# Group norms applied as they finish, and seven weight units inside a differential attention

## The reference, cut to what matters

```python
out_a = fox(...)   # causal softmax attention with forget gates, 4 heads of 64
out_b = mla(...)   # multi-head latent attention
out_c = stick(...) # stick-breaking attention
out_d = swa(...)   # sliding window, ALiBi, sinks
mix = concat([out_a, out_b, out_c, out_d])           # 4 groups of 256
y = group_rmsnorm(mix, mix_g) @ w_o                  # each group by its own rms
x = layernorm(ALPHA * x + y); x = layernorm(ALPHA * x + ffn(x))
```

```python
h = x + 0.5 * swiglu(rms_norm(x))
q, k, v, sc_b, sc_c, sc_x, lru_x, lru_g = split(rms_norm(h) @ w_in)
attn = softmax(q1 k1 + bias) - lam * softmax(q2 k2 + bias)   # 4 heads, 2 maps each
y_da = rms_norm(attn @ v, subln_g) * (1 - lam_init)          # each head by its own rms
y_sc = sc_b * causal_conv(sc_c * sc_x)
y_lru = gelu(lru_g) * rg_lru(conv(lru_x))                    # sigmoid gates, a scan over tokens
h = h + concat([y_da, y_sc, y_lru]) @ w_out
x = h + 0.5 * swiglu(rms_norm(h))
```

## Time and profile before

| | |
|---|---|
| median of 3 runs | 3333.64 us (3333.16 to 3333.65) |
| the profiled execution | 3340.57 us, its span 3338.5 us |
| TensorE busy | 3205.6 us, 96% |
| VectorE busy | 1540.4 us, 46% |
| ScalarE busy | 716.6 us, 21% |
| GpSimd busy | 1953.7 us, 59% |
| mean granted TensorE clock over the span | 0.974 |

### The profile page before, as it was taken

The page is one execution under the profiler, slowest core; times in us unless marked ns, Lnnn a source line. Parts: engine busy times, 40 slices in busy tenths (PEclk is TensorE's granted clock), DMA queues, the critical chain, the costliest instruction groups (busy, mean ns, idle before and its releaser), DMA issues.

```text
span 3338.5 us, 44718 instructions
## 1 busy us (share of the span) xinstructions
PE 3205.6 (96%) x15314; PEld 2621.4 (79%) x15314; DVE 1540.4 (46%) x1970; ACT 716.6 (21%) x1454; POOL 1953.7 (59%) x1566
## 2 busy tenths in 40 slices
PE   8998999989989999699999999999999999899998
PEld 7767888877768888588888668888888887588886
DVE  7567332285664331644326664432344236764422
ACT  3343110043522110411101331110111102421110
POOL 6223766653235666377766536776677666267763
PEclk9989999999989999899999999999999999899999
DMA  4111222221112222122223212222222232122221
GB/s 169 50 39 51 101 94 96 98 88 61 39 51 82 94 96 99 51 94 98 97 95 111 82 45 95 94 95 100 96 94 95 101 111 89 39 89 96 98 95 63
DMA packets 82021, 286.43 MB, mean 86 GB/s; under 512 B 9531, under 2 KB 13020, under 8 KB 81628
## 3 DMA queue, kind: packets, MB, share of 16 engines
q1 hardware_dynamic: 76032, 275.81, 24.5%
q10 hardware_dynamic: 5852, 8.78, 0.8%
HBM read 280.89 MB, written 3.67 MB: 85 GB/s over the span
## 4 chain that ended last, share of the span: by engine, by line
PE 90%; DVE 5%; issue 2%; ACT 2%; DMA 1%; ACTq 0%; DVEq 0%
PE bank_v L397 18%; PE bank_v L399 18%; PE bank_v L398 18%; PE bank_a L397 9%; PE bank_a L398 9%; PE bank_a L399 9%; PE bank_v L605 1%; PE bank_a L564 1%; PE bank_s L734 1%; PE bank_s L444 1%; PE bank_s L623 1%; ACT resid L933 1%; PE bank_v L587 1%; PE bank_a L436 0%; PE bank_s L631 0%
## 5 line engine op out<-in xcount | busy, mean ns | idle before, releaser
L371 POOL TENSOR_TENSOR w_lo<-raw,w_hi 128x1024 fp32r<-128x1024 f32 x520 | 1318.8, 2536 | 41.6
L368 POOL TENSOR_TENSOR zero<-zero 128x1 f32<-128x1 f32 x520 | 119.1, 229 | 1307.6 <-PE bank_v L399 975.9
L397 PE MATMUL bank_v<-xn_hi,w_hi 128*128 128x512 f32 (+1 forms) x1568 | 600.3, 383 | 7.5 <-POOL w_lo L371 2.8
L399 PE MATMUL bank_v<-xn_hi,w_lo 128*128 128x512 f32 (+1 forms) x1568 | 591.7, 377 | 0.0
L398 PE MATMUL bank_v<-xn_lo,w_hi 128*128 128x512 f32 (+1 forms) x1568 | 591.6, 377 | 0.0
L397 PE MATMUL bank_a<-xn_hi,w_hi 128*128 128x512 f32 (+1 forms) x1360 | 523.4, 385 | 40.3 <-DVE xn_lo L1283 21.5
L369 POOL CAST w_hi<-raw 128x1024 fp32r<-128x1024 f32 x520 | 549.0, 1056 | 0.0
L398 PE MATMUL bank_a<-xn_lo,w_hi 128*128 128x512 f32 (+1 forms) x1360 | 518.0, 381 | 0.0
L399 PE MATMUL bank_a<-xn_hi,w_lo 128*128 128x512 f32 (+1 forms) x1360 | 517.8, 381 | 0.0
L397 PE MATMUL bank_v<-h_hi,w_hi 128*128 128x512 f32 (+1 forms) x1100 | 419.7, 382 | 0.0
L399 PE MATMUL bank_v<-h_hi,w_lo 128*128 128x512 f32 (+1 forms) x1100 | 418.6, 381 | 0.0
(11 more groups left out here) (311 smaller groups left out, 3379.2 us busy)
## 6 DMA issues: line engine op xcount, KB each, us to landing
raw<-in_w_stream SPq DMA_DIRECT2D x520, 512.0 KB, 3.2
rope<-in_rope ACTq DMA_DIRECT2D x2, 1024.0 KB, 5.2
da_v<-t_rows ACTq DMA_DIRECT2D x2, 1024.0 KB, 5.8
out<-resid SPq DMA_DIRECT2D x4, 512.0 KB, 2.6
t_rows<-t_row ACTq DMA_DIRECT2D x1, 1536.0 KB, 5.7
resid<-in_x SPq DMA_DIRECT2D x4, 256.0 KB, 3.6
resid<-in_x ACTq DMA_DIRECT2D x4, 256.0 KB, 8.3
mla_v<-in_alibi ACTq DMA_DIRECT2D x2, 512.0 KB, 6.5
```

Source lines behind the costliest of these rows:

```text
L368: pool.tensor_tensor(zero[:, 1:2], zero[:, 0:1], zero[:, 0:1], ALU.add)
L371: pool.tensor_tensor(w_lo[:, u, :], raw[:, u, :], w_hi[:, u, :].bitcast(F32), ALU.subtract).then_inc(*w_split.done(("unit", u)))
L397: pe.matmul(out, lhs_hi, rhs_hi, start=first, stop=False)
L399: return pe.matmul(out, lhs_lo, rhs_hi, start=False, stop=last)
```

## The change

**First stack.** The fillers are spread over 25 steps in parts of two or three, in the order sq0, sk0, sq1, sk1, sv, wk, wq0, wq1. The norm factor of groups 0 and 1 is computed during the window attention (variance at step 22, diagonals at 25, broadcasts and scaled chunks at 27 and 28), that of group 2 at steps 30 to 32 and that of group 3 behind the attention. `project_out` opens three output units: their chunks 0 to 3, 4 and 5, and 6 and 7 run as the groups come, the third into `bank_s[2]`.

**Second stack.** The units `k2` 1 to 3, `q2` 2 and 3 and both `scb` are run as fillers inside the 16 steps of `diff`, in parts of half or a third; all `q2` go to `bank_v`. The gate matmuls stand right behind `scx`; `q2` 0 and `k2` 0 precede the values, `q2` 1 follows them. The turning lag is two steps. Values are ten 128x128 blocks a head. The short convolution runs on VectorE at steps 3 and 5 without `scb`, which is multiplied in at its eviction. The head norm is done for heads 0 to 2 together and for head 3 alone, around three opened units `wout` (the third in `stat_bank`) that begin with chunks 6, 7, 4 and 5. Several tiles share memory in another way, `lru_w` has a semaphore of its own, and the weight stream is reordered to match.

```diff
-FILLERS = (("sq", 0), ("sq", 1), ("sk", 0), ("sk", 1), ("sv", 0), ("sv", 1), ("sv", 2), ("sv", 3),
-           ("wq", 0), ("wq", 1), "wk")
+FILLERS = ((("sq", 0), 0, 3), (("sk", 0), 3, 6), (("sq", 1), 6, 8), (("sk", 1), 8, 10), (("sv", 0), 10, 12),
+           (("sv", 1), 12, 14), (("sv", 2), 14, 16), (("sv", 3), 16, 18), ("wk", 18, 20), (("wq", 0), 20, 22),
+           (("wq", 1), 22, 25))
+EARLY_ROWS = 2
+OPEN_OUTS = 3
+ROWS_STEP = 27
...
+DIFF_ITEMS = [(h, i) for h in range(4) for i in range(TT)]
+DIFF_LAG = 2
+DIFF_FILLERS = ((("k2", 1), 0, 2), (("q2", 2), 2, 4), (("k2", 2), 4, 6), (("q2", 3), 6, 8), (("k2", 3), 8, 10),
+                (("scb", 0), 10, 13), (("scb", 1), 13, 16))
+OPEN_ENDS = 3
+EARLY_CHUNKS = ((6, 7), (4, 5))
...
             def project_out(tag):
 
-                for c in range(DC - 2):
-                    project(("wo", c), v_bank, is_split("mixnorm") if c == 0 else None)
-                    if c == 2:
-                        ln_shift_sum(tag)
...
+                unit(("wo", 0))
+                chunks(0, range(0, 4))
+                early_sums("swa", added.after(("swa", "squares")), group_squares[:, 0, :])
+                unit(("wo", 1))
+                banks[1] = v_bank(("wo", 1))
+                chunks(1, range(0, 4))
+                chunks(0, range(4, 6))
+                chunks(1, range(4, 6))
+                mix_row(3)
+                unit(("wo", 2))
+                chunks(2, range(0, 6))
+                for c in range(OPEN_OUTS):
+                    chunks(c, range(6, 8)).then_inc(*w_used.done(("wo", c)))
+                for c in range(OPEN_OUTS, DC - 2):
+                    u = unit(("wo", c))
...
+                    if n == ROWS_STEP:
+                        for g in range(EARLY_ROWS):
+                            mix_row(g)
+                mix_row(2)
...
+                ready = {0: a_read.after(("v2", 2)), 1: v_read.after(("k2", 1)), 2: v_read.after(("k2", 2)),
+                         3: v_read.after(("k2", 3))}
...
+                for n in range(len(heads) + DIFF_LAG + 1):
+                    if n < len(heads):
+                        h, i = heads[n]
+                        if i == 0:
+                            pe.wait_ge(*ready[h])
+                        scores(heads[n])
+                    if head_ending_at(n - DIFF_LAG - 1) is not None:
+                        head_values(head_ending_at(n - DIFF_LAG - 1))
+                    filler(n)
+                    if DIFF_LAG <= n < len(heads) + DIFF_LAG:
+                        m = n - DIFF_LAG
+                        turn(("diff", *heads[m]), probs2[:, m % 4 * 2, :], heads[m][1] + 1)
+                    h = n // 4 - 2
+                    if n % 4 == 0 and h >= 0:
+                        early_sums(("subln", h), squared.after(("subln", h)), work[:, h, :])
+                    if n == len(heads):
+                        open_end(0)
+                    if n in (len(heads), len(heads) + 1):
+                        end_chunks(0, EARLY_CHUNKS[n - len(heads)])
+                for h in range(3):
+                    if h == 0:
+                        pe.wait_ge(*s_read.after(("diff", 3, TT - 1, 1)))
+                    head_row(h)
+                open_end(1)
+                end_chunks(1, EARLY_CHUNKS[0] + EARLY_CHUNKS[1])
+                early_sums(("subln", 3), squared.after(("subln", 3)), work[:, 3, :])
+                end_chunks(0, range(3))
+                end_chunks(1, range(3))
+                head_row(3)
+                open_end(2)
+                end_chunks(2, EARLY_CHUNKS[0] + EARLY_CHUNKS[1] + (0, 1, 2))
+                for c in range(OPEN_ENDS):
+                    end_chunks(c, (3,)).then_inc(*w_used.done(("wout", c)))
+                for c in range(OPEN_ENDS, DC):
+                    u = unit(("wout", c))
+                    b = v_bank(("wout", c))
+                    for k in range(DC):
+                        mm = mm3(b[:, :], *w_tile(u, k), mix_hi[:, k, :], mix_lo_of(k), k == 0, k == DC - 1)
...
-                for n in range(2):
-                    project(("scb", n), a_bank)
...
-                for n in range(4):
-                    project(("q2", n), a_bank)
-                pe.wait_ge(*par_in.after("tables2"))
...
-                    project(("k2", n), v_bank)
...
+                for c in range(2):
+                    pe.wait_ge(*lru_in.after("lru_w"))
+                    pe.wait_ge(*dve_step.after(("xr", c)))
...
+                project(("q2", 0), v_bank)
+                project(("k2", 0), v_bank)
                 project_rows("v2", 4, S)
...
-                pe.wait_ge(*dve_step.after(("q2", 3)))
+                project(("q2", 1), v_bank)
+                pe.wait_ge(*v_read.after(("k2", 0)))
+                pe.wait_ge(*v_read.after(("v2", 3)))
+                pe.wait_ge(*dve_step.after("t5_lo"))
                 diff()
...
                         early_add(group_at(n, 4))
+                    if n == 3 * GROUP_ITEMS - 2:
+                        mix_variance(0, EARLY_ROWS, a_read.after("mla"))
+                    if n == ROWS_STEP - 2:
+                        mix_diagonals(0, EARLY_ROWS)
+                    if n == ROWS_STEP + 1:
+                        for g in range(EARLY_ROWS):
+                            mix_apply(g)
+                        for g in range(EARLY_ROWS):
+                            mix_lo_group(g)
+                    if n == len(STREAM) - 2:
+                        mix_variance(2, 1, a_read.after("stick"))
+                    if n == len(STREAM):
+                        mix_diagonals(2, 1)
...
+                mix_apply(2)
                 early_add("swa")
-                dve.wait_ge(*a_read.after("swa"))
-                inverse_root("mixnorm", 4, 256, 1e-6, small)
-                apply_norm("mixnorm", 4, 2, lambda c: qmix[:, c, :], lambda c: col(par1, C1, "mix_g", c), xn_hi, xn_lo)
+                mix_lo_group(2)
+                mix_variance(3, 1, a_read.after("swa"))
+                mix_diagonals(3, 1)
+                mix_apply(3)
+                mix_lo_group(3)
...
-                for n in range(4):
-                    dve.wait_ge(*a_read.after(("q2", n)))
-                    dve.scalar_tensor_tensor(out=mix2[:, n, :], in0=mix2[:, n, :], scalar=HD ** -0.5, in1=scale_by[:, :],
-                                             op0=ALU.mult, op1=ALU.mult).then_inc(*dve_step.done(("q2", n)))
-                for n in range(4):
+                def keep_q(n):
+                    dve.wait_ge(*w_used.after(("q2", n)))
...
                                                   in1=lru_x[:, c, :], op0=ALU.mult, op1=ALU.mult), ("mult2", c))
+                keep_q(0)
+                keep_k(0)
...
-                    if n >= 5 and heads[n - 5][1] == TT - 1:
-                        h = heads[n - 5][0]
+                    h = head_ending_at(n - DIFF_LAG - 2)
...
                         keep(("diff", "out", h), sums, mix2[:, h, :])
-                dve.wait_ge(*a_read.after(("subln", 1)))
-                dve.wait_ge(*sums.after((("subln", 3), "sum")))
-                step(dve.tensor_copy(small[:, 2 * TT:4 * TT], stat_bank[:, 2 * TT:4 * TT]), ("subln", "sums"))
-                inverse_root("subln", 4, P, 1e-5, small)
-                apply_norm("subln", 4, 1, lambda c: mix2[:, c, :], lambda c: small[:, 127:128], mix_hi, mix_lo)
-                for c in range(4, DC):
-                    split_lo("subln", c, mix2[:, c, :], mix_hi, mix_lo)
+                    if n in (3, 5):
+                        short_conv((n - 3) // 2)
+                    if n in (4, 6):
+                        late_lo(6 + (n - 4) // 2)
+                    if n == 15:
+                        late_lo(4)
+                    if n == len(heads):
+                        head_variance(0, 3)
+                    if n == len(heads) + 1:
+                        head_diagonals(0, 3)
+                        late_lo(5)
+                for h in range(3):
+                    head_apply(h)
+                for h in range(3):
+                    head_lo(h)
+                head_variance(3, 1)
+                head_diagonals(3, 1)
+                head_apply(3)
+                head_lo(3)
```

402 lines of the change are left out of this document (277 added, 125 removed).

## The result

The changed kernel takes 3346.13 us, the median of 6 runs (3345.36 to 3346.49). The kernel before took 3333.64 beside it, 6 runs from 3331.03 to 3339.64. The ratio is 1.0029, with a 95% interval of 1.0019 to 1.0040. In a second comparison it was 1.0023 (1.0014 to 1.0032). Forecast were 3310 us and a range that ended at 3330. So the change makes the kernel slower by a quarter of a per cent, which no case of the prediction gave as its time; case 5, at 3342, is the nearest.

A forecast was written before the change was run, and what follows sets the result against it. TensorE, busy 96% of the span, was taken to bound the kernel. Gains of 11 us per block-1 layer and 1 per block-2 layer, two each, sum to 24: 3310 us beside the median 3333.6, range 3285 to 3330.

The forecast's parts named there:

- case 5: Rival, chance 0.07: GpSimd's splits stretch VectorE through block 2's differential attention, over 4.9 us per item; kernel slower, 3342.
- The tail of block 1: Block 1 behind the last values: 19.0 us to the third output unit's end, before 32.0; worth up to 13.0 us.
- (a): Block 1's tail still begins at half clock: some 5 us of matmuls, 2.5 lost, part of it lost before.
- Step (b): Block 1, step 28: four applies and four low parts, 5.8 us on VectorE, covered by its idle time of 4.13.
- case 4: Rival, chance 0.12: step 28 uncovered (block-1 gain 6), VectorE late in block 2's steps 3 to 7 (loss 6 per layer); 3334.
- (c): Block 1, step 32: ScalarE loads the root table ahead of the last copies; 1.3 us, or 2.7 by the Trainium skill.
- The fillers: Block 1: fillers take the same TensorE time over 25 steps as over 22; gain nothing.
- The bank wait of block 2: Before the value projection TensorE waits 10 us for VectorE's first query and key evictions, plus about 2.5 of half clock.
- the softplus: Block 2, VectorE ahead of the key eviction: softplus and its neighbours counted at 9.1 us.
- the case that the prediction priced at a wait of 5: Rival, chance 0.18: bank wait 5 us and block 2's tail half as long; block 2 gives 8 per layer, 3296.
- The steps with the convolutions: Block 2, steps 3 and 5: short convolutions delay the eviction the fourth query unit needs; 1.5 us, bounds 0 and 6.
- The tail of block 2: First end unit's chunk 5 waits for a low part behind twelve diagonals; tail loses 4.8 us (bounds 2 and 9).

## Why the prediction was wrong, point by point

**The tail of block 1: right.** Three opened units, one broadcast and the sums were priced at 19.0 us behind the last values. The shift matmul, four chunks of 0.68 into the fourth unit, starts at 276.19, so the third ended at 273.5: 19.2 us, without a wait. The half clock of (a) did not come: the granted clock was 1.00 from 254.29 on. Of the 13 us so won, 3 went further on: the layer norm's evictions were covered by nothing now, and TensorE waited 0.57, 1.05 and 0.59 us for them. The other 0.8 went in the same 150 matmuls; where, I did not trace.

**Step (b), "TensorE's steps there are 2 us, but VectorE has idle time to catch up in": this is the step that failed.** The sentence behind it gave the price, "if that cover were gone, it would cost all 5.8"; the wait was 6.00, and with the broadcasts, their 0.83 us wait, half clock and the root's table the last values came 8.8 us later, over the 4 that the prediction gave as the sign of case 4. The cover was read from the wrong step: the idle of 4.13 us stood before the row maximum of step 30, where TensorE has a pair's values to do. At step 29 nothing lies between row maximum, exponentials, copy and the next turned block, and VectorE's idle time there is its waiting for TensorE in that same loop. A piece put into it delays the loop by its whole length, 5.1 us for a wait that grew by 5.16. The row of the kernel before already said so: TensorE waited 0.84 us there for the copies, with nothing to spare. Around ScalarE's table load of (c) no further time shows: the copy before it ends at 247.52, the load runs from 247.54 to 248.82 and the root begins at 248.83, so (c) is the 1.3 of the sum and not the 2.7 given beside it. I had written this course down as case 4, with 0.12, and left 6 us of the gain to it where 1.3 were left.

**The fillers: wrong, to the good.** "The same TensorE time over 25 steps as over 22: nothing" left out the idle that they fill, 0.54 us a layer that can be seen; with what comes later, 0.4 to 3.2 us a layer between the profiles (217.3 and 217.6 for 218.1 to 220.5).

**The bank wait of block 2: right, and too long.** Forecast 10 us and 2.5 of half clock, measured 7.19 and about 2. The term that was too large is the softplus: "these rows are of the same steps with GpSimd as busy" did not hold. GpSimd idled for 6.1 us, from 1811.05 to 1817.15, while the softplus ran from 1813.12 to 1816.56, 3.4 us for the 9.1 counted; the table's low part, begun beside a split, took 4.22 for 2.3. The unstretched softplus is the case that the prediction priced at a wait of 5. (What stood ahead of the reciprocals in the kernel before was the scaling of all four queries, not of two, and the four keys.)

```profile
1808.97 4.22 DVE L1892 TENSOR_TENSOR t_lo<-da_v,t_hi 128x2048 fp32r<-128x2048 f32 x1
...
1817.15 0.20 POOL L422 TENSOR_TENSOR zero<-zero 128x1 f32<-128x1 f32 x1 [6.10 <-PE bank_v L453]
```

**The steps with the convolutions: right, too small.** The wait came where it was forecast, ahead of the fourth query unit in step 6 (the expectations above say step 8), as 2.81 us. Forecast 1.5 us in all, bounds 0 and 6; without the convolutions the attention was 5.5 and 5.2 us shorter. This is the other half of case 4.

**The tail of block 2: half right.** Chunk 5 waited 1.94 for 3 forecast (2.24 in the second layer). The eviction behind the first low part was not in the sum at all: 3.52 us and its clock, 5.1 to 6.7 in the run without it. With both waits gone the end units were 8.6 and 8.7 shorter. Opening a third unit brings three evictions close together, and nothing was asked of what VectorE does between them.

**The sum.** 11 for 1.3 in block 1 and 1 for -3.7 in block 2 make 29 us in the two pairs of layers; forecast -24 against the profiled execution, measured +4.8. The rest of the error, from +4.8 to the +12.5 between medians, is the 6.9 us by which I shifted both kernels, and 0.8 by which the changed kernel's profiled execution (3345.36) lay under its median: the kernel before takes 3331 to 3344 us from run to run and had been profiled in the upper part of that, and the changed one hardly varies (3344 to 3346). Step (b) is the largest part of the miss, but not all of it: with the applies spread the kernel took 3336.78, still above the range that ended at 3330.

**The rivals.** Case 4 had both mechanisms, step 28 and the steps of the convolutions, and put them at no change; what it lacked was the rest of block 1's loss and the eviction. Case 5 has the right sign and the wrong cause: VectorE is busy 57.18 of 80.95 us in the attention, 3.6 us an item and not over 4.9, and does not bound it. The slower outcome had 0.07 in all, too little for a change that adds work of VectorE at two places where TensorE waits for VectorE.

## What to carry to other kernels

An engine's idle time is cover only where it isn't itself waiting for the loop in which the new work would stand: before work is put there, follow one item round (scores, maximum, exponential, copy, turn) and see whether that round sets the pace at this step. Put it in small passes, one a step, behind what others wait for; the same eight passes cost the attention 4 to 5 us a layer in two pieces and nothing that shows one at a time. And gains read from one trace are spent once: idle time on VectorE that came from TensorE's stall was gone as soon as the stall was.

## What the runs showed of the hardware that I had not expected

An idle of TensorE costs more than its length, and not always the same. Two stretches of the changed kernel, behind the idle of 7.19 us and behind that of 3.52:

```profile
1829.60:1839.60 10.00, 9.91 (x33) 8.04 (x34) 6.37 (x8) 0.00 (x0) 1.62 (x3) 0.74 0.00 0
...
1973.40:1983.40 10.00, 9.93 (x37) 8.03 (x38) 7.62 (x8) 3.27 (x6) 9.68 (x8) 0.83 0.46 147
```

A clock of 0.74 over ten microseconds is a loss of 2.6 us, one of 0.83 a loss of 1.7. Behind the idle of 2.81 us too the clock was 0.50 for two microseconds, and had been 1.00 in the five before. The same 3.52 us wait was followed by 0.72 with the convolutions ahead, and by 1.00 and 0.73 in the two layers of the run with the low part first. Which it will be, the runs don't say.

Two passes of the convolution took 4.41 us while GpSimd split a unit beside them (its split of 2.72 us began at 1878.14) and 1.54 at 1889.68, behind the end of the next split. The Trainium skill ("SBUF — State Buffer", Who interferes with whom) says that VectorE and GpSimd can shut each other out for an instruction's whole length; these rows agree. The reciprocal of 128x512 took 3.35 us in all its 56 executions in the traces, beside GpSimd's splits too.
